# One blindly fetched expert gets two unrolled blocks, and the lightest expert moves into the loop's first turn

## What is computed

```python
def _hier_moe(x, w_group, b_group, w_router, b_router, w1, w3, w2):
    g_logits = (x @ w_group).astype(jnp.float32) + b_group
    grp = jnp.argmax(g_logits, -1)
    ...
    top_p, top_i = lax.top_k(jax.nn.softmax(e_logits, -1), TOP_K)
    ...
    eid = (grp[:, None] * EXPERTS_PER_GROUP + top_i).reshape(-1)
    ...
    def expert_block(args):
        xs, e = args
        return (jax.nn.silu(xs @ w1[e]) * (xs @ w3[e])) @ w2[e]
    ...
    return jax.ops.segment_sum(y, rows, num_segments=t + 1)[:t]
...
x = _layer_norm(DEEPNORM_ALPHA * x + moe, ln2_g[layer], ln2_b[layer])
```

## Time and profile before

| what | value |
|---|---|
| time, median of 3 runs | 2490.2 us (2490.2 to 2494.53) |
| the profiled execution's own time | 2489.88 us |
| its span | 2488.0 us |
| granted TensorE clock, mean over the span | 0.987 |
| PE busy | 2343.4 us, 94% |
| DVE / ACT / POOL busy | 43% / 34% / 6% |
| first matmul of the expert stage to its last | 1968 to 2453 us |
| blocks: scatters by POOL (line 967) | 37 |

### The profile page before, as it was taken

One profiled execution on the slowest core, in us unless ns is written; L12 is line 12 of the kernel. 1 busy time (PEld: TensorE's weight loads), 2 busy tenths in 40 slices (PEclk: granted clock), 3 DMA queues, 4 the chain that ended last, 5 costly groups with the idle time before them and its releaser, 6 DMA issues.

```text
span 2488.0 us, 28329 instructions
## 1 busy us (share of the span) xinstructions
PE 2343.4 (94%) x11582; PEld 1730.0 (70%) x11582; DVE 1062.1 (43%) x1712; ACT 852.2 (34%) x1258; POOL 155.2 (6%) x223
## 2 busy tenths in 40 slices
PE   7999999999999999999999999999999899999883
PEld 6768888888678888877777787887888533333321
DVE  4454222345553222557888885544234500000003
ACT  3354222234453222346666753334232111111112
POOL 1000000001000000000000000000001211111111
PEclk9999999999999999999999999999999999999997
DMA  9573332331534322233212213323235899999996
GB/s 344 217 279 102 102 102 77 128 140 36 232 105 136 101 93 86 87 94 97 60 47 68 81 35 100 98 68 101 69 102 221 318 417 417 416 416 416 416 416 267
DMA packets 215905, 442.13 MB, mean 178 GB/s; under 512 B 9588, under 2 KB 151076, under 8 KB 195808
## 3 DMA queue, kind: packets, MB, share of 16 engines
q1 hardware_dynamic: 206304, 419.52, 46.2%
q0 software_dynamic: 9472, 20.80, 2.4%
HBM read 435.55 MB, written 15.99 MB: 181 GB/s over the span
## 4 chain that ended last, share of the span: by engine, by line
PE 83%; DVE 5%; DMA 5%; ACT 3%; issue 2%; SPq 1%; DVEq 0%; POOL 0%; ACTq 0%; POOLq 0%
PE psum L1045 61%; PE psum L1730 9%; PE psum L1753 4%; DMA arena<-in_w 4%; PE psum L1480 1%; PE psum L1508 1%; PE psum L1076 1%; DMA arena<-in_ada_w 1%; PE psum L1500 1%; PE psum L1259 1%; SPq L760 1%; DVE arena L2937 0%; PE psum L1739 0%; DVE arena L3334 0%; ACT arena L1975 0%
## 5 line engine op out<-in xcount | busy, mean ns | idle before, releaser
L1045 PE MATMUL psum<-split,split 128*128 128x512 f32 (+3 forms) x7200 | 1602.8, 383 | 8.6 <-DVE split L2819 3.1
L1045 PEld LDWEIGHTS psum<-split,split 128*128 128x128 f32 x7200 | 1325.1, 189 | 260.6 <-issue 10.2
L2536 DVE TENSOR_TENSOR split<-arena,split 128x1024 fp32r<-128x1024 f32 x132 | 161.5, 1225 | 419.9 <-ACT split L1907 419.7
L1907 ACT ACTIVATE split<-arena 128x1024 fp32r<-128x1024 f32 x132 | 139.7, 1058 | 453.6 <-PE psum L1045 453.6
L1730 PE MATMUL psum<-arena 128*64 128x512 f32 x1184 | 268.4, 605 | 14.6 <-DMA arena<-in_w 13.9
L1730 PEld LDWEIGHTS psum<-arena 128*64 128x64 f32 x1184 | 99.3, 139 | 176.9 <-issue 156.0
L3334 DVE TENSOR_TENSOR arena<-arena,psum 128x256 f32<-128x256 f32 x37 | 15.6, 421 | 417.7 <-ACT arena L2364 417.7
L1753 PE MATMUL psum<-arena 128*64 128x512 f32 x592 | 135.2, 597 | 21.0 <-issue 19.8
L1753 PEld LDWEIGHTS psum<-arena 128*64 128x64 f32 x592 | 46.8, 136 | 85.6 <-issue 85.6
L2364 ACT ACTIVATE arena<-psum 128x256 f32<-128x256 f32 x37 | 14.2, 384 | 255.2 <-PE psum L1730 255.2
L2160 ACT ACTIVATE arena<-arena 128x1024 f32<-128x1024 f32 x56 | 58.4, 1055 | 63.9 <-DVE arena L2889 63.8
(11 more groups left out here) (387 smaller groups left out, 2030.4 us busy)
## 6 DMA issues: line engine op xcount, KB each, us to landing
arena<-in_w SPq DMA_DIRECT2D x96, 2048.0 KB, 26.4
arena<-in_w_in SPq DMA_DIRECT2D x56, 512.0 KB, 5.5
arena<-in_ada_w SPq DMA_DIRECT2D x24, 1024.0 KB, 8.5
arena<-in_ada_w SPq DMA_DIRECT2D x12, 2048.0 KB, 11.9
arena<-in_w_gate SPq DMA_DIRECT2D x22, 1024.0 KB, 5.5
arena<-in_w_up SPq DMA_DIRECT2D x22, 1024.0 KB, 8.0
arena<-in_w_down SPq DMA_DIRECT2D x12, 1536.0 KB, 6.4
arena<-in_w_in SPq DMA_DIRECT2D x16, 1024.0 KB, 6.4
```

The lines of the kernel that those rows point to most:

```text
L1045: m = nc.tensor.matmul(out, stationary(a), moving(b), start=start and n == 0, stop=stop and n == 2)
L1907: nc.scalar.activation(mlp_pieces[mlp_at(p)][:, 0], raw, ACT.Copy).then_inc(sem("mlp_hi"), 1)
L2536: v.tensor_tensor(mlp_pieces[mlp_at(p)][:, 1], mlp_raw(l, p)[1], mlp_pieces[mlp_at(p)][:, 0].bitcast(F32), ALU.subtract).then_inc(sem("mlp ...
```

## The change

In the key, experts 0 to 3 now stand in falling number: expert 3 at place 0, 2 at place 1, 1 at place 2, and 0 at place 3. The places with two unrolled blocks are 3 to 6 instead of 4 to 7 (`WIDE_AT`), so that expert 0 has two unrolled blocks and the three fullest of the others have two instead of the four fullest. They are served at q = 3, 8, 13 and 19. The unrolled list ends with place 30: place 31, the expert with the fewest rows, is served in the loop's first turn, at q = 31, and extra blocks come after it. STATIC is 35, and the loop's turns are the extra blocks plus one. Two DVE instructions of the key are gone from the routing's later part, and three that do the same stand ahead of a wait.

```diff
-ORDER = [0, 1, 2, 3, 4, 8, 9, 10, 11, 5, 12, 13, 14, 15, 6, 16, 17, 18, 19, 7, *range(20, EXPERTS)]
-BLOCKS = [(q, b) for q, p in enumerate(ORDER) for b in range(2 if FIXED <= p < FIXED + WIDE else 1)]
+WIDE_AT = FIXED - 1
+LOOP_Q = EXPERTS - 1
+ORDER = [0, 1, 2, 3, 7, 8, 9, 10, 4, 11, 12, 13, 14, 5, 15, 16, 17, 18, 19, 6, *range(20, EXPERTS)]
+BLOCKS = [(q, b) for q, p in enumerate(ORDER[:LOOP_Q]) for b in range(2 if WIDE_AT <= p < WIDE_AT + WIDE else 1)]
 STATIC = len(BLOCKS)
+PLANNED = STATIC + 1
-LOOP_Q = EXPERTS
-MAX_BLOCKS = STATIC + MAX_EXTRA
+MAX_BLOCKS = PLANNED + MAX_EXTRA
...
-        TAB_LOOP, TAB_TURNS = EXPERTS, EXPERTS + MAX_EXTRA
+        TAB_LOOP, TAB_TURNS = LOOP_Q, EXPERTS + MAX_EXTRA
...
-                e = q if q < FIXED else expert_at(ORDER[q])
+                e = FIXED - 1 - q if q < FIXED else expert_at(ORDER[q])
...
-                                             first_at[:, e, i], first_entry[:, i, e:e + 1], start=i == 0, stop=i == T - 1)
+                                             first_at[:, e, i], first_entry[:, i, FIRST - 1 - e:FIRST - e], start=i == 0, stop=i == T - 1)
...
+            C.link(v.tensor_scalar(key_bias, iota[:, 0:EXPERTS], float(FIXED), 2.0 ** 15, ALU.is_lt, ALU.mult))
+            C.settle()
+            C.link(v.scalar_tensor_tensor(out=key_bias, in0=iota[:, 0:EXPERTS], scalar=1.0, in1=key_bias, op0=ALU.add, op1=ALU.mult))
+            C.settle()
+            C.link(v.tensor_tensor(key_bias, key_bias, iota[:, 0:EXPERTS], ALU.subtract))
             dve.wait_ge(sem("routing_mm"), T)
...
-            C.link(v.tensor_scalar(key_bias, iota[:, 0:EXPERTS], -float(FIXED), 0.0, ALU.add, ALU.min))
-            C.settle()
-            C.link(v.scalar_tensor_tensor(out=key_bias, in0=key_bias, scalar=-2.0 ** 15, in1=iota[:, 0:EXPERTS],
-                                          op0=ALU.mult, op1=ALU.subtract))
...
-            C.link(v.scalar_tensor_tensor(out=over_e, in0=over_e, scalar=float(STATIC - 1), in1=base_e,
+            C.link(v.scalar_tensor_tensor(out=over_e, in0=over_e, scalar=float(PLANNED - 1), in1=base_e,
...
-            C.link(v.tensor_scalar(table_f[:, TAB_TURNS:], ends[:, EXPERTS - 1:EXPERTS], 1.0, None, ALU.max))
+            C.link(v.tensor_scalar(table_f[:, TAB_TURNS:], ends[:, EXPERTS - 1:EXPERTS], 1.0, None, ALU.add))
```

More of the change, by code:

```diff
@@ L101 @@
 FIRST, FIXED, WIDE = 3, 4, 4
-ORDER = [0, 1, 2, 3, 4, 8, 9, 10, 11, 5, 12, 13, 14, 15, 6, 16, 17, 18, 19, 7, *range(20, EXPERTS)]
-BLOCKS = [(q, b) for q, p in enumerate(ORDER) for b in range(2 if FIXED <= p < FIXED + WIDE else 1)]
+WIDE_AT = FIXED - 1
+LOOP_Q = EXPERTS - 1
+ORDER = [0, 1, 2, 3, 7, 8, 9, 10, 4, 11, 12, 13, 14, 5, 15, 16, 17, 18, 19, 6, *range(20, EXPERTS)]
+assert sorted(ORDER) == list(range(EXPERTS)) and ORDER[LOOP_Q] == LOOP_Q
+BLOCKS = [(q, b) for q, p in enumerate(ORDER[:LOOP_Q]) for b in range(2 if WIDE_AT <= p < WIDE_AT + WIDE else 1)]
 STATIC = len(BLOCKS)
+PLANNED = STATIC + 1
 LAST_BLOCK = {q: j for j, (q, _) in enumerate(BLOCKS)}
-LOOP_Q = EXPERTS
 LOOP_FREES = LOOP_Q - AHEAD
@@ L637, in rows_of @@
             q, b = BLOCKS[j]
-            return ORDER[q] + min(max(ORDER[q] - FIXED, 0), WIDE) + b
+            return ORDER[q] + min(max(ORDER[q] - WIDE_AT, 0), WIDE) + b
         block = ctx.enter_context(nc.Block())
@@ L784, in _ @@
                     sp.wait_ge(sem("routing_dve"), TABLE)
-                e = q if q < FIXED else expert_at(ORDER[q])
+                e = FIXED - 1 - q if q < FIXED else expert_at(ORDER[q])
                 expert_up(e, q, free[0:2])
                 expert_down(e, q, free[2])
-            turns = sp.value_load(table_i[0:1, TAB_TURNS:TAB_TURNS + 1].bitcast(I32), min_val=1, max_val=MAX_EXTRA)
+            turns = sp.value_load(table_i[0:1, TAB_TURNS:TAB_TURNS + 1].bitcast(I32), min_val=1, max_val=MAX_EXTRA + 1)
             with sp.Fori(0, turns) as i:
@@ L1007, in _ @@
             pool.wait_ge(sem("routing_dve"), TABLE)
-            turns = pool.value_load(table_i[0:1, TAB_TURNS:TAB_TURNS + 1].bitcast(I32), min_val=1, max_val=MAX_EXTRA)
+            turns = pool.value_load(table_i[0:1, TAB_TURNS:TAB_TURNS + 1].bitcast(I32), min_val=1, max_val=MAX_EXTRA + 1)
             with pool.Fori(0, turns) as i:
@@ L1771, in _ @@
             pe.wait_ge(sem("routing_dve"), TABLE)
-            turns = pe.value_load(table_i[0:1, TAB_TURNS:TAB_TURNS + 1].bitcast(I32), min_val=1, max_val=MAX_EXTRA)
+            turns = pe.value_load(table_i[0:1, TAB_TURNS:TAB_TURNS + 1].bitcast(I32), min_val=1, max_val=MAX_EXTRA + 1)
             with pe.Fori(0, turns) as i:
@@ L2385, in _ @@
             act.wait_ge(sem("routing_dve"), TABLE)
-            turns = act.value_load(table_i[0:1, TAB_TURNS:TAB_TURNS + 1].bitcast(I32), min_val=1, max_val=MAX_EXTRA)
+            turns = act.value_load(table_i[0:1, TAB_TURNS:TAB_TURNS + 1].bitcast(I32), min_val=1, max_val=MAX_EXTRA + 1)
             with act.Fori(0, turns) as i:
@@ L3215, in _ @@
             dve.wait_ge(sem("routing_dve"), ONEHOTS)
-            C.link(v.tensor_tensor(first_entry, m_sum[:, 0:T, 0:FIRST],
+            C.link(v.tensor_tensor(first_entry, m_sum[:, 0:T, FIXED - FIRST:FIXED],
                                    entries[:, 0:T].rearrange("p (t a) -> p t a", a=1).to_broadcast([P, T, FIRST]), ALU.mult))
@@ L3224, in _ @@
             for e in range(FIRST):
-                v.tensor_tensor(first_at[:, e], over_tiles(row_rank, CAP), rank[:, :, e:e + 1].to_broadcast([P, T, CAP]),
+                v.tensor_tensor(first_at[:, e], over_tiles(row_rank, CAP), rank[:, :, FIXED - 1 - e:FIXED - e].to_broadcast([P, T, CAP]),
                                 ALU.is_equal).then_inc(sem("routing_dve"), 1)
@@ L3243, in _ @@
             C.settle()
-            C.link(v.tensor_scalar(wide_e, place, float(FIXED + WIDE), None, ALU.is_lt))
-            C.link(v.tensor_scalar(base_e, place, -float(FIXED), 0.0, ALU.add, ALU.max))
+            C.link(v.tensor_scalar(wide_e, place, float(WIDE_AT + WIDE), None, ALU.is_lt))
+            C.link(v.tensor_scalar(base_e, place, -float(WIDE_AT), 0.0, ALU.add, ALU.max))
             C.settle()
-            C.link(v.scalar_tensor_tensor(out=wide_e, in0=place, scalar=float(FIXED), in1=wide_e,
+            C.link(v.scalar_tensor_tensor(out=wide_e, in0=place, scalar=float(WIDE_AT), in1=wide_e,
                                           op0=ALU.is_ge, op1=ALU.mult))
@@ L3349, in _ @@
             dve.wait_ge(sem("routing_dve"), TABLE)
-            turns = dve.value_load(table_i[0:1, TAB_TURNS:TAB_TURNS + 1].bitcast(I32), min_val=1, max_val=MAX_EXTRA)
+            turns = dve.value_load(table_i[0:1, TAB_TURNS:TAB_TURNS + 1].bitcast(I32), min_val=1, max_val=MAX_EXTRA + 1)
             with dve.Fori(0, turns) as i:
```

## The result

The changed kernel takes 2473.95 us (median of 4 runs, 2472.05 to 2476.15) beside 2490.64 for the kernel before (4 runs). The ratio is 0.9925, interval 0.9913 to 0.9938: by the ratio 18.7 us less of 2490, by the two medians 16.7. Two later series of the same pair, with more runs of before beside them, gave 0.9941 (0.9929 to 0.9953) and 0.9938 (0.9925 to 0.9951), 14.7 and 15.4 us less. The forecast was 12.4 us less, 2477.8, with 2472.0 as the lowest time: the direction and the bound of the stage held, the size was too small, and the first series lies just inside the low edge of the range as a time and beyond it as a ratio (0.9925 x 2490.2 = 2471.6).

A forecast was written before the change was run, and what follows sets the result against it. The DMA's bytes after 1976 us, plus PE's work after the last landing, were taken to bound the end. Removing the turn gains 13.9 us, later landings cost 1.5: 12.4 less, 2477.8 us, range 2472.0 to 2485.0.

The forecast's parts named there:

- the sum: Whole kernel: 13.9 - 1.5 = 12.4 us off the profiled 2489.88, plus 0.3 for the median, gives 2477.8 us.
- How the numbers follow: Odds and range for the whole kernel: 2472.0 to 2485.0 us; faster 0.94, same 0.04, slower 0.02.
- Part 1: End of the expert stage: the extra block and its weight load go, a gain of 13.9 us less d.
- rival C: Last expert's load in small pieces runs at a lone DMA's lower rate: 2479.0 us, 2481.1 by the skill's table; chance 0.05.
- Part 2: Middle of the expert stage: q = 3's second block delays q = 6's loads, so the DMA pauses 1.5 us.
- The term for bytes: Expert 0's 51-row scatter moves from behind the weights to ahead of them: 0.21 MB, costing 0.5 us.
- d: How much later weight landings of a given q come than before: 1.5 + 0.5 - 0.5 = 1.5 us.
- Rival B: Stock of issued loads at q = 3 isn't usable as counted, so a longer pause: 2482.5 to 2488.8 us; chance 0.07.
- Part 3: Start of the expert stage: block 0 gathers 8 rows instead of 64, saving 0.5 us, within 0 to 2.88.
- The tail: After the last scatter to the span's end: 34.9 us, which the change leaves as it is.
- Rival A: All uncertain falls well: no pause, no wait for block 0's gather, q = 30 at full clock: 2472.2 us; chance 0.07.
- The signs of being wrong: Over 4 us of pause at 2026, a DMA wait inside the loop's block, 37 scatters, or landings moved over 4 us.

The follow-up runs named there:

- e1: Changed kernel with double blocks back at q = 4, 9, 14, 19, expert 0's rows 65 to 115 left out, `y_rows` filled mid-kernel: 2480.08 us, ratio 0.9958.
- e6: Changed kernel with its second and third double block one turn later (q = 3, 9, 14, 19): 2476.58 us, ratio 0.9943.
- e7: Changed kernel with double blocks at q = 2, 3, 8, 13 and first experts in order 2, 1, 0, 3: 2488.41 us, ratio 0.9992.
- e3: Changed kernel with only three places with two blocks, so 35 blocks and the same 32 loads: 2477.75 us, ratio 0.9945.
- e4: Changed kernel with all 32 experts unrolled again and an empty loop turn, 37 blocks and 33 loads: 2493.23 us, ratio 1.0005.

## Why the prediction was right or wrong

- **The step that failed** is the sum, which takes the profiled execution's 2489.88 us less 12.4, and so sets everything ahead of the expert stage at no change, since it is "the same program"; and with it the range in "How the numbers follow", whose low end holds only what can vary in the expert stage and takes the spread between executions into account at the high end alone. The part ahead is the same in its instructions but not in its time: 4.3 us in the first pair of traces. Block 0 started between 1962.99 and 1968.98 us in the eleven other profiled executions of this study (the latest is e1's, with its filling), and in the trace that I worked from at 1968.45.
- **Term by term,** the first pair of traces gives 17.8 us where the sum had 12.4. The 5.4 between them are: part ahead of the stage 4.3 (I had 0), gather 1.0 (0.5), clock in q = 30's block 1.7 (0), tail 0.9 (0), and against these pause and bytes 4.0 (2.0). So two errors partly cancelled. The mechanism of the gain was right; the sizes of the small terms were not.
- **Chance between series** has a part in the 18.7 us: the changed kernel's first four times have a median of 2473.95, its later series 2477.54 and 2476.34. The trace of before was no slow one as a whole: 2489.88 beside a median of 2490.64, though its block 0 started late.
- **What moves block 0's start** is in part the granted clock ahead of it. Summed over stretches of 4 us up to 1960 (the missing share of the clock times 4 us, stretches below 0.97), it lacks 10.2 us in the first trace of before, 5.1 in the first of the changed kernel, and 1.7 in e6's, which has the earliest start of all. The order isn't strict (5.0 in e7's, which starts at 1966.79), and the two traces of piece 1 show one reason: the same loss costs 1.6 us or nothing, by whether a wait takes it up.
- **The bound** (the DMA's bytes, then what PE does after the last landing) was right. e3 takes a block away and gains nothing; e7 leaves the 36 blocks and 32 loads and loses 12 us by letting the DMA wait.
- **Part 1, 13.9 us for the turn,** was right, and so was its cause: e4, with the spare turn back, is at 1.0005. The loop's load of q = 31 was in time, and its pieces of 1.05 MB cost nothing (408 to 422 GB/s from 2411 to 2425 us of the changed kernel), so rival C and the Trainium skill's table beside it ("DMA: Bandwidth & Descriptors", Bandwidth) did not come true in a full queue.
- **Part 2, the pause,** was the right mechanism at the right place (2020 to 2024, by the earlier start 5 us ahead of my 2026), but too small: 2.3 us, not 1.5. The term for bytes failed more: 1.4 us by q = 24, not 0.5. I had counted only the scatter of expert 0's second block, and not its gather, which before came as late as 2412 us; e1 gives 3.5 us for both against my 2.0 (3.3 expected after the result). The sum also took 0.8 us off the pause for rows that come early. They do (1.33 MB instead of 1.00 in the first 50.3 us from SP's first issue), but bytes ahead of the landings delay them as a pause does, and in d they had to stand too. Rival B's size was far off here and its mechanism real, as e7 shows.
- **Part 3, the gather,** 0.5 us said; the wait is 1.75 to 1.87 us in the three traces of the changed kernel against 2.88 and 2.21 before, so 0.3 to 1.1, some 0.7. With 2.22 in e3 for the same 8 rows, part of this is chance.
- **The tail** I had left as it is; it is 0.5 to 1.0 us shorter in the three traces of the changed kernel (34.0, 33.9 and 34.4, against 34.9 in both of before). What part is the smaller last scatter and what part the emptier DMA wasn't tried, and e6 with the same last scatter has 34.7.
- **Rival A's clock** came true in two of three traces of the changed kernel: q = 30's block ran at full clock after the same idle time. I had excluded it by a pattern of alternating waits which a shift of all landings should leave alone. This argument failed: the same wait of 2.38 us was followed by either duration.
- **The sum, put right:** 13.9 - 3.7 + 0.7 (gather) + 0.9 (tail) = 11.8 us, if q = 31's block before runs at full clock and q = 30's after at half, as the prediction had it. With both at the same clock it is 1.7 more, 13.5 (11.7 in the stage and 1.6 around it, 13.3, by the pairs). With q = 31's block slow before, as in the second trace, and q = 30's at full clock after, it is 15.2. The clock in block 0 adds or takes another 1.4. So the chance of the clock alone spreads the gain from 11.8 to 15.2 us and more. The two repeated series, 14.7 and 15.4 with about 3 us to either side, agree with that; the first, 18.7 with 3, only just. Why all three lie at the upper end or above it I can't say, and an effect of the change of 1 to 3 us ahead of the expert stage isn't excluded by three traces of the one kernel and two of the other.
- **The signs of being wrong** that the prediction named: the pause was 2.3 us and not over 4, no wait for DMA stands inside the loop's block, there are 36 scatters. Only the landings came close to their limit of 4 us: 4.0 later at q = 24 and 3.9 at q = 30, counted from block 0.

## What to carry to other kernels

Where a stage is bound by loads that are queued ahead, count bytes and the moments at which the queue runs dry, not blocks of compute: a spare load at the end costs its own bytes and the compute behind it, and it can be the whole price of a loop that must run once. Holding a buffer for one block (12.45 us) more was free where the load ahead ended 20 us after the old issue (q = 8: 2108.6, by the prediction's working, against 2088.66), and cost 2.3 us where it landed 13.5 us after it (q = 3: 2027.4 against 2013.95). And a range for a saving of half a per cent needs the spread between executions on both sides, from more than one trace if there is one.
